# A gated delta rule's head outputs: normalised and gated by VectorE straight from PSUM, instead of after a ScalarE copy

## The reference, cut to what matters

```
o  = gated_delta_rule(q, k, v, g, beta)          # 16 value heads, 128 wide, chunks of 64
zg = silu(z.reshape(B, S, 16, 128))
o  = rmsnorm(o, norm_w) * zg                     # over the 128 values of each head, eps 1e-6
return o.reshape(B, S, 2048) @ w_out
# rmsnorm(x, w) = x * rsqrt(mean(x*x) + eps) * w
```

## Time and profile before

| what | value |
|---|---|
| median of 3 executions | 1620.57 us (1618.72 to 1621.36) |
| the profiled execution's own time | 1621.4 us |
| its span in the trace | 1619.6 us |
| PE busy | 1554.8 us, 96% of the span |
| DVE busy | 1109.9 us, 69% |
| ACT busy | 932.7 us, 58% |
| POOL busy | 493.4 us, 30% |
| step i = 3 of the heads loop (258.10 to 273.38 us) | 15.28 us |

### The profile page before, as it was taken

One profiled execution on the slowest core, in us unless ns is written; L12 is line 12 of the kernel. 1 busy time (PEld: TensorE's weight loads), 2 busy tenths in 40 slices (PEclk: granted clock), 3 DMA queues, 4 the chain that ended last, 5 costly groups with the idle time before them and its releaser, 6 DMA issues.

```text
span 1619.6 us, 37025 instructions
## 1 busy us (share of the span) xinstructions
PE 1554.8 (96%) x13269; PEld 1429.3 (88%) x13269; DVE 1109.9 (69%) x2304; ACT 932.7 (58%) x1763; POOL 493.4 (30%) x405
## 2 busy tenths in 40 slices
PE   7899999899999999999999999999999999999998
PEld 6899877798998899888999999999999888888886
DVE  3787768656556653776478888798888555555554
ACT  1766567744555555545354444799898544555554
POOL 4000278661000040000067777766565100000000
PEclk9999979899999999999999999999999999999999
DMA  9668412454443344247455555544444666666663
GB/s 295 219 184 278 150 55 82 133 163 130 151 131 118 111 156 131 79 157 156 104 150 167 168 168 172 162 143 135 140 131 143 182 194 194 193 192 190 194 193 127
DMA packets 211832, 255.89 MB, mean 158 GB/s; under 512 B 15912, under 2 KB 193804, under 8 KB 211724
## 3 DMA queue, kind: packets, MB, share of 16 engines
q1 hardware_dynamic: 211723, 254.39, 53.2%
HBM read 253.29 MB, written 1.05 MB: 157 GB/s over the span
## 4 chain that ended last, share of the span: by engine, by line
PE 72%; DVE 11%; issue 5%; DMA 4%; ACT 4%; SPq 2%; DVEq 0%; ACTq 0%
PE ps L2253 22%; PE ps L2861 22%; PE ps L2843 10%; PE ps L2831 3%; DMA raw<-in_u_experts 3%; PE ps L2273 2%; PE ps L2551 2%; DVE raw L2014 2%; SPq L580 2%; PE ps L2628 1%; DVE w_lo L1396 1%; PE ps L2451 1%; DMA arena<-in_ada_w 1%; DVE arena L2067 1%; PE ps L2648 1%
## 5 line engine op out<-in xcount | busy, mean ns | idle before, releaser
L742 POOL TENSOR_TENSOR w_lo<-raw,w_hi 128x1024 fp32r<-128x1024 f32 x128 | 307.6, 2406 | 337.7 <-ACT w_hi L1265 337.6
L2253 PE MATMUL ps<-x_hi,w_hi 128*128 128x256 f32 x1088 | 315.3, 290 | 8.3 <-DVE w_lo L1396 3.0
L2253 PE MATMUL ps<-x_hi,w_lo 128*128 128x256 f32 x1088 | 308.2, 283 | 0.0
L2253 PE MATMUL ps<-x_lo,w_hi 128*128 128x256 f32 x1088 | 308.2, 283 | 0.0
L2212 DVE TENSOR_TENSOR w_lo<-raw,w_hi 128x1024 fp32r<-128x1024 f32 x124 | 152.0, 1226 | 143.2 <-ACT w_hi L1374 143.2
L1374 ACT ACTIVATE w_hi<-raw 128x1024 fp32r<-128x1024 f32 x124 | 131.6, 1061 | 168.0 <-PE ps L2861 168.0
L2253 PEld LDWEIGHTS ps<-x_hi,w_hi 128*128 128x128 f32 x1088 | 209.1, 192 | 15.3 <-issue 6.0
L2253 PEld LDWEIGHTS ps<-x_lo,w_hi 128*128 128x128 f32 x1088 | 209.2, 192 | 1.3 <-issue 1.2
L2253 PEld LDWEIGHTS ps<-x_hi,w_lo 128*128 128x128 f32 x1088 | 209.0, 192 | 0.0
L1265 ACT ACTIVATE w_hi<-raw 128x1024 fp32r<-128x1024 f32 x128 | 134.9, 1054 | 113.4 <-DVE raw L2014 113.2
L2806 PE MATMUL ps<-x_hi,w_hi 128*128 128x256 f32 x576 | 166.3, 289 | 10.6 <-ACT arena L1287 9.7
(11 more groups left out here) (446 smaller groups left out, 3563.7 us busy)
## 6 DMA issues: line engine op xcount, KB each, us to landing
raw<-in_u_experts SPq DMA_DIRECT2D x512, 128.0 KB, 2.7
raw<-in_v_experts SPq DMA_DIRECT2D x128, 512.0 KB, 4.3
arena<-in_ada_w SPq DMA_DIRECT2D x18, 1024.0 KB, 7.8
raw<-in_a_w_in SPq DMA_DIRECT2D x12, 1024.0 KB, 5.7
arena<-in_a_w_in SPq DMA_DIRECT2D x12, 1024.0 KB, 5.7
raw<-in_b_w_in SPq DMA_DIRECT2D x8, 1024.0 KB, 5.7
arena<-in_b_w_in SPq DMA_DIRECT2D x8, 1024.0 KB, 5.6
raw<-in_w_in SPq DMA_DIRECT2D x8, 1024.0 KB, 5.6
```

What stands on the lines that cost most here:

```text
L742: pool.tensor_tensor(UTL[e], UT[e % 2], UTH[e].bitcast(F32), ALU.subtract).then_inc(utl_ready, 1)
L2253: ins = mm(o[:, b * S:b * S + S], w[:, slot, kk, b * P:b * P + P], xx[:, (kk + turn) % KC, :], start=(kk == 0 and n == 0), stop=(kk == k - ...
```

## The change

- ScalarE no longer copies `A2[g]` to `OS[g]`. `finish_out` becomes `finish_squares`, with the squares alone. Its wait for the previous round's outputs (`h_out`) moves to `finish_norms`.
- VectorE gets a new step `gated(r)`: for each head it waits until the square is done and then multiplies `A2[g]` (PSUM) by the norm's weights and the gate, in place over the gate in `ZB`. It signals `h_os`. It stands behind `mask_level(i, 4)` and ahead of `lowers(n)`.
- `normed` is one product instead of two: `ZB` by `RNo[g]`, in place.
- TensorE's `finish(r, 5)`, which overwrites the other half of the PSUM bank, waits for `h_os` too.
- The semaphore `h_og` is used by `remainder` alone.

```
             def finish_squares(r):
+                for g in range(2):
+                    act.wait_ge(h_o, r.nth(g))
+                    act.activation(SQo[g], A2[g], ACT.Square).then_inc(h_sq, 1)
+            def finish_norms(r):
                 if r.at:
                     act.wait_ge(h_out, r.count(2, 2))
-                for g in range(2):
-                    act.wait_ge(h_o, r.nth(g))
-                    act.activation(OS[g], A2[g], ACT.Copy).then_inc(h_os, 1)
-                    act.activation(SQo[g], A2[g], ACT.Square).then_inc(h_sq, 1)
...
+            def gated(r):
                 if r.at >= 6:
                     v.wait_ge(z_late, 1)
+                for g in range(2):
+                    v.wait_ge(h_sq, r.nth(g))
+                    zb = ZB[:, r.heads[g], :]
+                    v.scalar_tensor_tensor(zb, A2[g], COLS[:, CAN:CAN + 1], zb, ALU.mult, ALU.mult).then_inc(h_os, 1)
+
+            def normed(r, g):
                 v.wait_ge(h_orn, r.nth(g))
                 v.wait_ge(h_os, r.nth(g))
-                v.scalar_tensor_tensor(OS[g], OS[g], COLS[:, CAN:CAN + 1], RNo[g], ALU.mult, ALU.mult).then_inc(h_og, 1)
-                v.wait_ge(h_og, r.nth(g, 1, 1, 2))
                 zb = ZB[:, r.heads[g], :]
-                v.tensor_tensor(zb, OS[g], zb, ALU.mult).then_inc(h_out, 1)
+                v.tensor_tensor(zb, zb, RNo[g], ALU.mult).then_inc(h_out, 1)
...
                 close_level(i, 3)
                 mask_level(i, 4)
+                if f:
+                    gated(f)
                 if n:
                     lowers(n)
...
             remainder(Round(GQ - 1))
+            gated(Round(GQ - 1))
             for g in range(2):
                 normed(Round(GQ - 1), g)
...
                     elif step == 3:
-                        pe.wait_ge(h_og, r.nth(g, 1, 0, 2))
+                        pe.wait_ge(h_og, r.nth(g))
...
                     else:
                         pe.wait_ge(h_sq, r.nth(g))
+                        pe.wait_ge(h_os, r.nth(g))
                         mm(B2[g], ones, SQo[g], start=True, stop=True).then_inc(h_oss, 1)
```

More of the change, by code:

```diff
@@ L973, in finish_second, with finish_squares @@
                     act.activation(VN[g][:, 128:256], B2[g][:, 128:256], ACT.Copy).then_inc(h_c3, 1)
-            def finish_out(r):
+            def finish_squares(r):
+                for g in range(2):
+                    act.wait_ge(h_o, r.nth(g))
+                    act.activation(SQo[g], A2[g], ACT.Square).then_inc(h_sq, 1)
+            def finish_norms(r):
                 if r.at:
                     act.wait_ge(h_out, r.count(2, 2))
-                for g in range(2):
-                    act.wait_ge(h_o, r.nth(g))
-                    act.activation(OS[g], A2[g], ACT.Copy).then_inc(h_os, 1)
-                    act.activation(SQo[g], A2[g], ACT.Square).then_inc(h_sq, 1)
-            def finish_norms(r):
                 for g in range(2):
@@ L1009, in inner @@
                 if f:
-                    finish_out(f)
+                    finish_squares(f)
                 spread(i, 0)
@@ L1038, in _ @@
             finish_second(Round(GQ - 1))
-            finish_out(Round(GQ - 1))
+            finish_squares(Round(GQ - 1))
             finish_norms(Round(GQ - 1))
@@ L1682, in remainder @@
                                            BV[r.side][g][:, 128:256], ALU.mult, ALU.add).then_inc(h_og, 1)
-            def normed(r, g):
+            def gated(r):
                 if r.at >= 6:
                     v.wait_ge(z_late, 1)
+                for g in range(2):
[3 more added lines that the diff above has]
+            def normed(r, g):
                 v.wait_ge(h_orn, r.nth(g))
                 v.wait_ge(h_os, r.nth(g))
-                v.scalar_tensor_tensor(OS[g], OS[g], COLS[:, CAN:CAN + 1], RNo[g], ALU.mult, ALU.mult).then_inc(h_og, 1)
-                v.wait_ge(h_og, r.nth(g, 1, 1, 2))
                 zb = ZB[:, r.heads[g], :]
-                v.tensor_tensor(zb, OS[g], zb, ALU.mult).then_inc(h_out, 1)
+                v.tensor_tensor(zb, zb, RNo[g], ALU.mult).then_inc(h_out, 1)
             def modulator(r):
```

## The result

The changed kernel took 1632.21 us (median of 13, 1622.14 to 1633.97), the kernel before 1620.57 us beside it (13, 1618.16 to 1622.08). The ratio is 1.0060, 95% interval 1.0046 to 1.0073: slower by about 0.6%. The forecast was 1621.4, range 1618.5 to 1624.8, with 0.16 for slower. The profiled execution's own time was 1631.68 us, its span 1630.0.

The account below looks back on a forecast made before the run. The chain lay on TensorE for 72%, VectorE 11%, ScalarE 4%, with VectorE setting half of each step. Terms 1.35 + 0 + 0.46 - 0.95 = +0.86 us on 1620.57 gave 1621.4 us, range 1618.5 to 1624.8.

Parts of the forecast that it names:

- the steady step: Heads loop, steps 1 to 5: VectorE's +0.78 for `gated` less 0.51 for L1689 gives +0.27 us each, +1.35 in all.
- The rival that `gated` itself is held up: Heads loop: GpSimd slows each `gated` product to 0.83 us, sum +5.3, 1625.8 us; chance 0.07.
- TensorE's side of the steady step: `level_d(5)` ends later, so `close_level(5)` could start at 278.76 against 278.54: +0.22 us, below VectorE's +0.27.
- The clock: Rival: a longer VectorE half pauses TensorE and its clock falls; one more fall costs +3.8 us, 1625.2; chance 0.10.
- step 6: Step ending on ScalarE's table loads and L965: VectorE's delay of 0.3 us is covered, 0; without cover +0.27.
- step 7: Step without `norm_sums` or GpSimd work: `close_level(5)` starts at 327.90 instead of 327.44, +0.46 us (0.34 to 0.64).
- `gated`: 0.79 us for the pair: VectorE's half: each product lasts 458 ns and adds 0.39 us, 0.78 for the pair (0.66 to 0.96).
- The gain from `mask_level(5)` to `close_level(5)`: VectorE's half: `normed(f, 0)` loses its first product L1689, saving 0.51 us, while L1692 keeps its 0.72.
- ScalarE's copies: Two copies a step removed from ScalarE, worth nothing, since the squares stay 0.8 us ahead of VectorE's `gated`.
- The new wait of TensorE: `finish(f, 5)` waits for `gated`, done at 273.84 and 274.23, before its matmul's turn at about 274.4: free.
- The 0.95 us behind the loop: Behind the heads loop: one product per head lets `lo` begin 1.2 us earlier; TensorE uses 0.95, so -0.95 us.
- a sign of being wrong: Prediction wrong if `lowers` or L1692 change by over 0.2 us, `gated` exceeds 0.6, or the clock drops in steps 2 to 5.

Follow-up runs that it names:

- E6: The changed kernel without GpSimd's tree of sums, its signals sent at once: 1620.35 us, ratio 0.9989 to the kernel before with its tree.
- E9: The changed kernel with GpSimd's tree of sums waiting until VectorE's `lowers` pair is done, all work kept: 1623.27 us, ratio 1.0002 to the kernel before.
- E5: The changed kernel with three identity products in TensorE's pause ahead of `setup_low`, steps 1 to 5 only: 1628.13 us, ratio 1.0037 to the kernel before.
- E12: The changed kernel unchanged, run again for a second profile: 1632.03 us, ratio 1.0061 to the kernel before.
- E1: The kernel before with two additional unread VectorE products of 128x256 from PSUM behind the fourth mask: 1635.7 us, ratio 1.0087.
- E14: The kernel before with two additional PSUM products behind the fourth mask and GpSimd's tree waiting for `lowers`: 1624.82 us, ratio 1.0017.
- E15: E9's kernel with ScalarE's copy of each head's output put back, read by nobody: 1623.32 us, ratio 1.0004 to the kernel before.
- E13: The kernel before with GpSimd's tree of sums waiting until the `lowers` pair is done: 1626.29 us against 1622.20, ratio 1.0020.
- E11: The changed kernel with first head's `gated` ahead of the fourth mask, `normed(f, 0)` moved to the next step, tree waiting for `lowers`: 1622.67 us, ratio 0.9998.
- E2: The changed kernel with six identity products put into TensorE's pauses in each step: 1631.68 us, ratio 1.0058 to the kernel before.

## Why the prediction was wrong

**The step that failed** is that of the steady step: "They are held instead by `lowers` and `close_level(4)`, which move by 0.78, but that is what I have just counted." I moved `lowers` by 0.78 us and kept its 1.25 us. But these are two products with both inputs in SBUF, and GpSimd's tree begins just then. The runs showed 1.61 us in its place, and 0.75 where GpSimd is kept away (E6, E9). With that the step grew by 0.76 us, not by 0.27, and TensorE got a pause of 0.73 us that the sum did not have. The prediction named the spread of 426 to 839 ns and read it as GpSimd's doing, but used it for L1692 alone. The rival that `gated` itself is held up was wrong: L1689 took 474 to 484 ns in all sixteen cases. It was the neighbour that `gated` pushed.

By size this is the smaller part. The medians lie 11.6 us apart; the five longer steps are 3.8 of it, of which `lowers` has 5 x 0.36 = 1.8. The larger part is a term that the sum put at nothing: further falls of TensorE's clock, 8.4 us in the profiled execution. The four executions at 1622.14 to 1624.89 us, with the higher granted clock, lie for the most part inside the forecast's range of 1618.5 to 1624.8, so by them the longer steps alone would hardly have left it; E5, 6.3 us above the kernel before without these falls, says otherwise, and this stays open.

**Another term was missing**: `level_p(0)` of the next step, 0.45 us, stands behind `level_d(5)` in TensorE's queue, and `mask_level(0)` needs it. I followed TensorE's side only to `close_level(5)`. The 0.09 us above fits this: `level_p(0)` ended at 290.08, `mask_level(0)` began at 290.16.

**A row was misread**: `close_level(5)` started at 278.46, as VectorE's timeline has it; the 278.54 of the earlier trace rows is where its piece of the chain begins. TensorE's side of the steady step is then +0.30 instead of +0.22, and not VectorE's +0.27 but this side sets the step. The sum moves by 0.15 us. The timeline of the kernel before:

```profile
278.46 0.41 DVE L1674 TENSOR_SCALAR arena<-ps 64x256 f32<-64x256 f32 x1
278.79 0.20 DVE L1653 TENSOR_TENSOR arena<-ps,arena 128x64 f32<-128x64 f32 x1
```

**The clock** was a rival, at 0.10, with one fall at 3.8 us. It came true in the first profile twice in steps 1 to 5, at 4.2 us each. My case against it was one longer step that had held 1.00, and an addition of 0.3 us; the addition was 0.76, with TensorE's new pause of 0.73 us. E5 shows that filling this pause removes these falls: its profile has none in steps 1 to 5, and its five executions had a mean granted clock of 0.985 to 0.988. Each of the three falls in steps 1 to 5 of the changed kernel's two profiles began right behind such a pause: it ended at 228.80, 266.21 and, in E12, 296.03, and the windows of 1 us that first show a granted clock below 1.00 are those from 229, 266 and 296. The same pause in the other steps brought no fall. The executions say the same of `lowers`. Where it takes 1.61 us and the pause is open, the mean granted clock was 0.981 or less in 9 of 13 executions of the changed kernel, 4 of 6 in E12 and 3 of 6 in E1; where the tree waits for it (E9, E14, E15) in none of 36. What makes the clock fall in one execution and not in the next stays open, and so does the length of pause that it takes: E9 had a fall at shorter steps, and E1, with the longest steps, only one in its profile.

**The account of the profiled executions** (span +10.4 us). From the first `mask_level(4)` to the last, the loop took 129.41 us instead of 117.67, +11.7. Of that 2 x 4.2 = 8.4 are falls in steps 1 to 5, and 5 x 0.76 = 3.8 longer steps. The low spell ahead of step 1 was 1.2 us cheaper, step 6, at the low clock for the most part in both, cost 0.8 more. Ahead of the loop's first mask the changed kernel was 1.3 us later, where the two kernels do not differ, and behind the last 2.7 us quicker, of which I can name the 0.95 of TensorE's idle time.

**Steps 6 and 7.** For step 6 the forecast was 0, because ScalarE's table loads cover the delay. They did but for 0.20 us: L965 started 8.51 us behind `mask_level(4)` instead of 8.32, now behind TensorE. The rest of the 0.8 no run explains. For step 7 it was +0.46. From `mask_level(4)` to `close_level(5)` it took 5.71 us instead of 4.01, but there the changed kernel's profile has the low clock and that of the kernel before the full one, so the term itself was not measured.

**What was right.** `gated`: 0.79 us for the pair, forecast 0.78; 474 ns each, forecast 458. The estimate by the page VectorE: DVE Perf Modes of the Trainium skill (section on the trn2 errata), 0.55 us each and 1.09 the pair, was too high; the measurement decides. The gain from `mask_level(5)` to `close_level(5)` was 0.50 us, forecast 0.51 for L1689, but that is luck: the product that stays took 0.42 us instead of the 0.72 that I kept, and the 0.24 us for which VectorE waits for `level_d(5)` took most of this back. ScalarE's copies: nothing (E15). The new wait of TensorE: nothing on the path. The 0.95 us behind the loop: idle time gone. Over the program L1695 took 417 ns as a median, where L1692 took 720; the prediction had named a change of more than 0.2 us there, and in `lowers`, as a sign of being wrong, and both came.

That a VectorE product with two SBUF inputs and a GpSimd instruction that reads SBUF exclude each other is what the page SBUF — State Buffer of the Trainium skill (section Who interferes with whom) says; the trace agrees for `lowers` (0.75 us alone, 1.25 beside L683, 1.61 beside L691), and `gated`, with one SBUF input, ran free beside GpSimd. I had cited the rule for the instructions that change and not for those that only move.

## What to carry to other kernels

When a change delays an instruction, look up what the other engines are doing at its new place, not only what it waits for. A product with two SBUF inputs has one duration alone and another beside GpSimd, and a shift of 0.8 us can turn the one into the other in every step of a loop. Where this is the loss, a wait on the engine with time to spare can remove it (E9), but the same wait elsewhere can make a collision (E13): it has to be placed by the timelines of both engines. And when the sum of a change is small, look whether it opens a pause on TensorE: here the falls of the clock that came with a pause of 0.73 us cost 8.4 us in the profiled execution, and the longer steps themselves 3.8.

## What the runs showed of the hardware

- In the steady steps two VectorE products of 128x256 with both inputs in SBUF took 0.75 us alone, 1.25 beside GpSimd's 128x128 products, 1.61 beside its 128x256 products; E11, with the first of them partly clear, 1.02.
- A scalar_tensor_tensor of 128x256 from PSUM with one SBUF input took 474 to 484 ns in all sixteen cases, beside GpSimd's L683 in the steady steps too. The same form with both inputs in SBUF took 474 to 829.
- The clock's falls in this loop differ between executions of one kernel (two in steps 1 to 5, then one), and the changed kernel's times lie in two groups, 1622.14 to 1624.89 us and 1630.23 to 1633.97, while those of the kernel before, in the same series, spread over 1618.16 to 1622.08.
- Products of the identity put into the loop to hold the clock lengthened the steps that lie partly at the low clock: steps 0 and 6 of E2 took 21.7 and 22.1 us, those of the changed kernel 19.1 or 20.3 and 20.5.
